# Blocks of the split expert weights moved from 2048-byte steps to steps of 2112 and 2128 bytes

## The reference

```python
def moe_ffn(x, w_r, wg, wu, wd):
    logits = jnp.dot(xt, w_r)
    top_v, top_i = lax.top_k(logits, TOP_K)          # 2 of 8 experts
    w = jax.nn.softmax(top_v, axis=-1)
    ...
    for e in range(N_EXPERTS):
        h = jax.nn.silu(xt @ wg[e]) * (xt @ wu[e])    # 1024 -> 3584
        y = y + gates[:, e:e + 1] * jnp.dot(h, wd[e]) # 3584 -> 1024
```

## Time and profile before

| | |
|---|---|
| median of 3 runs | 1535.66 us (1535.2 to 1539.36) |
| span of the profiled execution | 1535.8 us |
| TensorE busy, share of the span | 99% |
| DVE, ACT busy | 80%, 65% |
| mean granted TensorE clock | 0.997 |
| HBM read | 429.4 MB |

### The profile page before, as it was taken

The page is one execution under the profiler, slowest core; times in us unless marked ns, Lnnn a source line. Parts: engine busy times, 40 slices in busy tenths (PEclk is TensorE's granted clock), DMA queues, the critical chain, the costliest instruction groups (busy, mean ns, idle before and its releaser), DMA issues.

```text
span 1535.8 us, 21611 instructions
## 1 busy us (share of the span) xinstructions
PE 1527.8 (99%) x8428; PEld 1333.0 (87%) x8428; DVE 1234.4 (80%) x1253; ACT 998.9 (65%) x1079; POOL 217.5 (14%) x249
## 2 busy tenths in 40 slices
PE   9999999999999999999999999999999999999998
PEld 7989999999998988888888888888888888888887
DVE  5877666654477758988988888998998988898897
ACT  5655433333466547777777778777777777777775
POOL 5514400001150403101001001002002002002000
PEclk9999999999999999999999999999999999999999
DMA  8333455444443459999999999999999999999994
GB/s 226 96 110 116 149 164 164 133 157 151 125 122 110 141 209 367 383 366 388 372 381 376 374 374 376 391 359 386 384 363 382 381 362 379 400 361 363 394 373 183
DMA packets 159701, 437.43 MB, mean 285 GB/s; under 512 B 12068, under 2 KB 66176, under 8 KB 145264
## 3 DMA queue, kind: packets, MB, share of 16 engines
q1 hardware_dynamic: 151796, 423.02, 75.0%
q0 software_dynamic: 5552, 9.62, 2.3%
q10 hardware_dynamic: 2252, 3.41, 0.7%
HBM read 429.40 MB, written 13.60 MB: 288 GB/s over the span
## 4 chain that ended last, share of the span: by engine, by line
PE 98%; DMA 0%; ACT 0%; DVE 0%; issue 0%; SPq 0%; DVEq 0%; ACTq 0%
PE bank L1981 34%; PE bank L2475 13%; PE bank L2484 13%; PE bank L2479 13%; PE bank L2510 6%; PE bank L2513 6%; PE bank L2519 6%; PE bank L1984 3%; PE bank L2528 2%; PE bank L2496 0%; PE bank L2502 0%; PE bank L2495 0%; DMA gla<-b_g 0%; DVE x L1972 0%; ACT L1076 0%
## 5 line engine op out<-in xcount | busy, mean ns | idle before, releaser
L1808 DVE TENSOR_TENSOR split_lo<-raw,split_hi 128x2048 fp32r<-128x2048 f32 x336 | 763.1, 2289 | 101.8 <-ACT split_hi L1207 100.8
L1207 ACT CAST split_hi<-raw 128x2048 fp32r<-128x2048 f32 x336 | 640.5, 1911 | 224.5 <-PE bank L2484 145.7
L2475 PE MATMUL bank<-split_hi,xgT_hi 128*128 128x512 f32 x896 | 291.7, 395 | 0.0
L2479 PE MATMUL bank<-split_hi,xgT_lo 128*128 128x512 f32 x892 | 285.8, 390 | 0.0
L2484 PE MATMUL bank<-split_lo,xgT_hi 128*128 128x512 f32 x896 | 239.9, 390 | 0.0
L913 ACT CAST cut_hi<-ring 128x1024 fp32r<-128x1024 f32 x124 | 129.9, 1048 | 166.6 <-PE bank L1981 166.6
L1981 PE MATMUL bank<-xT_hi,cut_hi 128*128 128x320 f32 x752 | 236.7, 315 | 0.0
L1981 PE MATMUL bank<-xT_hi,cut_lo 128*128 128x320 f32 x752 | 233.5, 310 | 0.0
L1981 PE MATMUL bank<-xT_lo,cut_hi 128*128 128x320 f32 x752 | 231.9, 308 | 0.0
L1346 DVE TENSOR_TENSOR cut_lo<-ring,cut_hi 128x1024 fp32r<-128x1024 f32 x124 | 153.0, 1235 | 80.7 <-ACT cut_hi L913 79.9
L2484 PEld LDWEIGHTS bank<-split_lo,xgT_hi 128*128 128x128 f32 x896 | 168.3, 188 | 34.9
(11 more groups left out here) (316 smaller groups left out, 1723.2 us busy)
## 6 DMA issues: line engine op xcount, KB each, us to landing
raw<-moe_w_gate SPq DMA_DIRECT2D x112, 1024.0 KB, 7.8
raw<-moe_w_up SPq DMA_DIRECT2D x112, 1024.0 KB, 7.6
raw<-moe_w_down SPq DMA_DIRECT2D x112, 1024.0 KB, 7.3
ring<-w_in SPq DMA_DIRECT2D x15, 1024.0 KB, 5.5
ring<-ffn_w_gate SPq DMA_DIRECT2D x11, 1024.0 KB, 5.5
ring<-ffn_w_up SPq DMA_DIRECT2D x11, 1024.0 KB, 5.4
ring<-ffn_w_down SPq DMA_DIRECT2D x10, 1024.0 KB, 5.1
ring<-w_out SPq DMA_DIRECT2D x8, 1024.0 KB, 5.0
```

What stands on the lines that cost most here:

```text
L1207: return nc.scalar.copy(split_hi[:, i % SR, :], raw_piece(i)).then_inc(hi_ready, 1)
L1808: V.tensor_tensor(split_lo[:, i % SR, :], raw_piece(i), split_hi[:, i % SR, :].bitcast(F32), ALU.subtract).then_inc(lo_ready, 1)
L2475: TE.matmul(o, xgT_hi[:, kk, :], hi[:, w * k + 512 * c:w * k + 512 * c + 512], start=kk == 0, stop=False)
L2479: TE.matmul(o, xgT_lo[:, kk, :], hi[:, w * k + 512 * c:w * k + 512 * c + 512], start=False, stop=False)
```

## The change

The two tiles get a dimension for the block of 512 columns, with a pitch of 528 (2112 bytes) in `split_hi` and 532 (2128 bytes) in `split_lo`; the columns behind each 512 are never used. ACT and DVE now write four runs of 512 in one instruction instead of one of 2048, DVE also reads `split_hi` so, and `raw` is described to them as four adjoining runs. The matmuls read the same 512 columns of the same blocks in the same order.

```diff
+HI_W, LO_W = 528, 532
...
-        split_hi = sb("split_hi", [P, SR, PIECE], FR)
-        split_lo = sb("split_lo", [P, SR, PIECE], FR)
+        split_hi = sb("split_hi", [P, SR, 4, HI_W], FR)
+        split_lo = sb("split_lo", [P, SR, 4, LO_W], FR)
...
+        def raw_blocks(i):
+            return raw_piece(i).rearrange("p (b n) -> p b n", b=4)
+
+        def hi_blocks(i):
+            return split_hi[:, i % SR, :, 0:512]
+
+        def lo_blocks(i):
+            return split_lo[:, i % SR, :, 0:512]
...
-                return nc.scalar.copy(split_hi[:, i % SR, :], raw_piece(i)).then_inc(hi_ready, 1)
+                return nc.scalar.copy(hi_blocks(i), raw_blocks(i)).then_inc(hi_ready, 1)
...
-                V.tensor_tensor(split_lo[:, i % SR, :], raw_piece(i), split_hi[:, i % SR, :].bitcast(F32), ALU.subtract).then_inc(lo_ready, 1)
+                V.tensor_tensor(lo_blocks(i), raw_blocks(i), hi_blocks(i).bitcast(F32), ALU.subtract).then_inc(lo_ready, 1)
...
-                    hi, lo = split_hi[:, i % SR, :], split_lo[:, i % SR, :]
+                    hi, lo = hi_blocks(i), lo_blocks(i)
...
-                                TE.matmul(o, xgT_hi[:, kk, :], hi[:, w * k + 512 * c:w * k + 512 * c + 512], start=kk == 0, stop=False)
+                                TE.matmul(o, xgT_hi[:, kk, :], hi[:, len(ms) * k + c, :], start=kk == 0, stop=False)
```

More of the change, by code:

```diff
@@ L2469, in experts @@
                     if j < 2 * FC:
-                        n, w = 4 // len(ms), 512 * len(ms)
+                        n = 4 // len(ms)
                         outs = [banks[2 * up + (FC * h + m) % 2][:] for m in ms]
@@ L2478, in experts @@
                             for c, o in enumerate(outs):
-                                TE.matmul(o, xgT_lo[:, kk, :], hi[:, w * k + 512 * c:w * k + 512 * c + 512], start=False, stop=False)
+                                TE.matmul(o, xgT_lo[:, kk, :], hi[:, len(ms) * k + c, :], start=False, stop=False)
                         pe.wait_ge(lo_ready, ip * (2 * NP) + (i + 1 + PR))
@@ L2483, in experts @@
                             for c, o in enumerate(outs):
-                                last = TE.matmul(o, xgT_hi[:, kk, :], lo[:, w * k + 512 * c:w * k + 512 * c + 512], start=False, stop=kk == KB - 1)
+                                last = TE.matmul(o, xgT_hi[:, kk, :], lo[:, len(ms) * k + c, :], start=False, stop=kk == KB - 1)
                         if first and i == 0:
@@ L2488, in experts @@
                                 for c, o in enumerate(outs):
-                                    last = TE.matmul(o, xgT_lo[:, k, :], hi[:, w * k + 512 * c:w * k + 512 * c + 512], start=False, stop=False)
+                                    last = TE.matmul(o, xgT_lo[:, k, :], hi[:, len(ms) * k + c, :], start=False, stop=False)
                     elif q == NP - 1:
@@ L2493, in experts @@
                                 b = FEB - 2 + k
-                                c = slice(1024 * k + 512 * n, 1024 * k + 512 * n + 512)
-                                TE.matmul(banks[6 + n][:], hmT_hi[:, b, :], hi[:, c], start=False, stop=False)
-                                TE.matmul(banks[6 + n][:], hmT_lo[:, b, :], hi[:, c], start=False, stop=False)
+                                c = 2 * k + n
+                                TE.matmul(banks[6 + n][:], hmT_hi[:, b, :], hi[:, c, :], start=False, stop=False)
+                                TE.matmul(banks[6 + n][:], hmT_lo[:, b, :], hi[:, c, :], start=False, stop=False)
                             if n == 0:
@@ L2500, in experts @@
                                 b = FEB - 2 + k
-                                c = slice(1024 * k + 512 * n, 1024 * k + 512 * n + 512)
-                                last = TE.matmul(banks[6 + n][:], hmT_hi[:, b, :], lo[:, c], start=False, stop=k == 1)
+                                c = 2 * k + n
+                                last = TE.matmul(banks[6 + n][:], hmT_hi[:, b, :], lo[:, c, :], start=False, stop=k == 1)
                             if n == 0:
@@ L2508, in experts @@
                             for n in range(2):
-                                c = slice(1024 * k + 512 * n, 1024 * k + 512 * n + 512)
-                                TE.matmul(banks[6 + n][:], hmT_hi[:, b, :], hi[:, c], start=b == 0, stop=False)
+                                c = 2 * k + n
+                                TE.matmul(banks[6 + n][:], hmT_hi[:, b, :], hi[:, c, :], start=b == 0, stop=False)
                             for n in range(2):
-                                c = slice(1024 * k + 512 * n, 1024 * k + 512 * n + 512)
-                                TE.matmul(banks[6 + n][:], hmT_lo[:, b, :], hi[:, c], start=False, stop=False)
+                                c = 2 * k + n
+                                TE.matmul(banks[6 + n][:], hmT_lo[:, b, :], hi[:, c, :], start=False, stop=False)
                         pe.wait_ge(lo_ready, ip * (2 * NP) + (i + 1 + PR))
@@ L2517, in experts @@
                             for n in range(2):
-                                c = slice(1024 * k + 512 * n, 1024 * k + 512 * n + 512)
-                                last = TE.matmul(banks[6 + n][:], hmT_hi[:, b, :], lo[:, c], start=False, stop=b == FEB - 1)
+                                c = 2 * k + n
+                                last = TE.matmul(banks[6 + n][:], hmT_hi[:, b, :], lo[:, c, :], start=False, stop=b == FEB - 1)
                     last.then_inc(piece_used, 1)
```

## The result

The changed kernel takes 1554.51 us (1553.65 to 1557.13, four runs) against 1535.66: the ratio is 1.0116, with a 95% interval of 1.0104 to 1.0129. It is 18.9 us slower, outside the stated range of 1529 to 1543 and on the side to which the prediction had given a chance of 0.10.

A forecast was written before the change was run, and what follows sets the result against it. The prediction took TensorE's distance between matmul starts in the expert part to bound the kernel. Its terms summed to 0 us against the profiled 1535.8, so it forecast the median, 1535.7 us, with an 8-in-10 range of 1529 to 1543.

The forecast's parts named there:

- What bounds the kernel: Expert part: the distance between matmul starts on TensorE, 226.7 ns, sets the time; ACT, DVE and DMA follow its pace.
- ACT's copy and DVE's subtraction in four runs: Expert part's splits: writing four runs costs ACT 0 ns and DVE 0 to 10 ns, judged from rows of similar kind.
- Rival 3: Expert part: DVE becomes the bound if each run's start costs it 0.15 us; 47 us slower, 1583 us, chance 0.02.
- the matmuls' moving reads: Expert part's matmuls: count, widths, order and waits stay, so the new block offsets change their time by 0 us.
- Two widths: Matmuls of 512 and 320 columns: one column per cycle plus 13.4 ns each, so no collision cost growing with columns.
- the fixed 13.4 ns: Each matmul's time beyond one column per cycle, claimed equal at 512 and 320 columns.
- Two layouts: Dense part's moving blocks step 1280 bytes through eight offsets within 2048, yet pay the same 13.4 ns: many offsets gain nothing.
- Rival 1: Each matmul's 13.4 ns are a meeting with the next weight load; faster, 1518 us for a third gone, chance 0.10.
- With and without writers: Expert part: matmuls take 227.5 ns mostly without ACT writing, 226.3 under ACT and DVE; difference only rounding.
- The shift by 1728 bytes of the tiles behind: Stationary tiles xgT_hi, xgT_lo, hmT_lo: their load is in the shadow and their block spacing stays, so 0 us.
- Rival 2: Expert matmuls: moving starts off a multiple of 256 bytes cost 4.7 ns each; 15 us slower, 1551 us, chance 0.08.
- The prediction's last sentence: Matmuls: the prediction is wrong if the fixed cost depends on offsets finer than 256 bytes, untested by any row.

The follow-up runs named there:

- the map: Separate kernel of matmuls alone, 128 to 512 columns, moving and weight starts varied: at 320 columns, 146.6 to 146.7 ns at start differences of 0, 64, 128 and 192.
- f1: Changed kernel, but from the fourth piece on ACT and DVE split only the first 8 columns of each block: 1555.43 us, one run.
- s1: Kernel before, blocks still 2048 bytes apart, but split_lo 768 bytes later and all tiles behind it 1728 bytes later: 1547.36 us, ratio 1.0069.
- a1: Kernel before with 64 bytes of padding ahead of hmT_hi, so moving blocks and their weights start 64 bytes later together: 1537.75 us, ratio 1.0000.
- w1: Kernel before with 128 bytes of padding ahead of xgT_hi, no moving block moved: 1554.62 us, ratio 1.0112.
- the first map: Separate kernel of 49 groups of 64 matmuls alone, each group with its own moving and weight offsets: 226.7 ns with both at 64, 233.4 with moving 192, weights 0.
- the third map: Separate kernel of 512-column matmuls alone, starts alternating or stepping from one to the next: 231.7, 228.4 and 231.6 ns with both starts stepping together.

## Why the prediction was wrong

**What bounds the kernel** was right, and it is why every nanosecond counts: TensorE without idle time, ACT and DVE and the DMA queue behind it. The runs show the same picture in all versions.

**ACT's copy and DVE's subtraction in four runs**, 0 and 0 to 10 ns: right, 1912 and 2289 ns against 1911 and 2289. **Rival 3** is out with them. One of the rows behind them was misread, though: in the rotary sum `xhat<-t` only the output is broken into eight runs, and its two inputs are 384 adjoining columns each. It said nothing of DVE's broken read of `split_hi`; that this read costs nothing the changed kernel's 2289 ns show, and the row did not.

**The step that failed is "the matmuls' moving reads: 0 us, by the three readings".** Each reading was a correct row with a conclusion that it couldn't carry.

1. *Two widths.* The slope and the fixed 13.4 ns are right, but both rows show matmuls in a state where distance costs nothing: 512 columns at a distance of 0, and 320 columns, which pay at no distance. They say nothing of 512 columns at another distance.
2. *Two layouts.* I counted the dense part's offsets within 2048 bytes; 1280 is five times 256, so each of its tiles has one offset only, within 256. Rival 1 says as much ("the steps are still multiples of 256 bytes, and the new ones are not"), and the sum didn't draw the consequence. Its distances aren't 0 either (`hT_hi` starts at 96 and `cut_hi` at 128), but at 320 columns none of the four distances of the map costs anything. So the row I took as the test of the change's idea tested it where it has no effect. This is the most expensive sentence of the prediction, and the profile couldn't have shown it: no row of before has 512 columns at another distance. What could have been seen is that the two parts differ in more than the offsets.
3. *With and without writers.* Right, and f1 confirms it, but it excluded the wrong partner. What the stream's time depends on is where TensorE's own weight loads read, and these accompany every matmul, so they can't be seen by comparing stretches.

**"The shift by 1728 bytes of the tiles behind: 0 us"** failed too. s1 measured that shift alone at 1.0069, about 11 us. The load being in the shadow (PEld 166.7 of 200 us) hides its length, not where it reads.

**Rival 2** had the right side, a time near the right one (1551 us) and the wrong mechanism. The moving block's start alone doesn't count here: a1 moved all of them from 64 to 128 at no cost, and w1 lost 17 us without moving any. That its estimate came close is an accident: it took the 231.4 ns of the matmuls behind a transpose as price, which happens to be near the 230.8 and 233.3 ns of the change's pieces. It had a chance of 0.08 although the prediction says that no row of before could test it; an effect that nothing tests should have had much more. The prediction's last sentence, on offsets finer than 256 bytes, names the sign of being wrong that came.

**Rival 1.** The fixed 13.4 ns stay at the best distance. No offset that the maps tried at 512 columns gives less, in 16-byte steps up to 128 and coarser ones beyond, and so the kernel before is already at the lowest time seen. No version ran faster than it. At 256 columns and a distance of 192 the rest over 106.7 ns of columns is 6.6 ns instead of 13.9, so the 13.4 ns are not fixed for every width.

**The sentences from the Trainium skill.** The one on lines of 16 bytes (SBUF — State Buffer, the box on cachelines) supported 0 us for Rival 2. Against it, the first map has the moving start at 16 bytes (L59) at 231.7 ns and the second has both at 16 more than a multiple of 32 (both at 48, L97) at 229.8 but both at 32 (L96) at 226.9; a line of 16 bytes would make no difference between these. The same skill says that the moving stream and the weight load have independent read ports and that loading the next weights doesn't steal bandwidth from the running matmul (TensorE: Matmul & The Clock Gate, "Step-by-step: what each phase is for"). Against it speak 2.4 to 6.7 ns a matmul of 512 columns at distances of 64, 128 and 192, where nothing but the two starts differs. Whether the 226.7 ns at 0 are free of the load no run shows, since none has matmuls without one.

The arithmetic of the change itself closes: 1.9% fewer matmuls in each 200 us, 18 us in the expert part, 18.9 between the medians and 18 by the ratio of 1.0116. What stays open is the mechanism below the distance. The maps, in which ACT and DVE do nothing beside the matmuls, show that the starts of TensorE's two reads are enough to make the cost. That the two reads meet in the memory, and in which part of it, is only argued, from the period of 256 bytes.

## What to carry to other kernels

Where TensorE is the bound, look at the start addresses of both its operands. For 512 float32r columns with a fresh weight load, keep the moving start and the weights' start equal within 256 bytes, at a multiple of 64, and the same from one matmul to the next (equal starts that step together by 64 to 192 cost 1.6 to 5.0 ns each in the third map). Pad other tiles by multiples of 256: a tile of the wrong size far ahead in the allocation can cost 0.7% to 1.1% by shifting the weights alone. A row that shows no effect is evidence only for its own shape, so before a null result is carried from one stage to another, list all that differs between them.

## What the hardware showed that I had not expected

- With starts that stay the same and are multiples of 64 bytes, the time of a 512-column matmul goes by distance within 256 bytes: 226.7 ns at 0, 229.1 at 64, 232.3 at 128, 233.4 at 192, and repeats at 256.
- Equal starts are not enough: both at 16 take 230.0 ns, and both alternating between 0 and 64 take 231.7.
- It goes by the number of columns in no simple way: nothing at 320, a gain of some 7 ns at 256 columns and a distance of 192 (113.3 against 120.6 at 0).
- One matmul at another distance puts up to seven behind it off the pace, at 46 ns in all, its own part included, in the worst case seen. With the start alternating, 0 and 192 cost 227.0 on average.
- Writes of ACT and DVE to the tiles that TensorE reads cost it nothing: 894 matmuls in 200 us with 149 and 175 us of their work as with 32 of each.
